# Both MLPs of a two-block model as one level of Strassen's scheme

## What is computed

```python
# first block
m = rmsnorm(h, norm_mlp[i])
h = h + jnp.square(jax.nn.relu(m @ w_up[i])) @ w_down[i]          # 1024 x 4096, 4096 x 1024
gate = jax.nn.sigmoid(rmsnorm(h, norm_ple[i]) @ w_ple_gate[i])
h = h + gate * (p[i] @ w_ple_proj[i])
# second block
h2 = rms_norm(x, norm_mlp_g[l])
x = x + jnp.square(jax.nn.relu(h2 @ w_up[l])) @ w_down[l]
```

## Time and profile before

| what | value |
|---|---|
| median of 3 runs | 2806.08 us (2803.96 to 2809.75) |
| profiled execution, its own time | 2805.16 us |
| its span | 2803.4 us |
| mean granted TensorE clock | 0.988 |
| TensorE busy | 2681.8 us, 96% |
| DVE, ACT, POOL busy | 1376.1, 601.4, 1122.2 us |
| HBM read, written | 123.36, 8.39 MB |

### The profile page before, as it was taken

How to read it: one execution, slowest core, us unless ns; L and a number is a source line. 1 busy time by engine, 2 the same in 40 slices (tenths; PEclk the granted TensorE clock), 3 DMA queues, 4 the chain that set the end, 5 groups by cost and what they waited for, 6 DMA issues and landing times.

```text
span 2803.4 us, 32575 instructions
## 1 busy us (share of the span) xinstructions
PE 2681.8 (96%) x13042; PEld 2207.0 (79%) x13042; DVE 1376.1 (49%) x1457; ACT 601.4 (21%) x713; POOL 1122.2 (40%) x617
## 2 busy tenths in 40 slices
PE   7889999899999999999998999999999999999997
PEld 6657787787788888888876788887778888888885
DVE  5677456554533322333457576667664323333234
ACT  3253313322201100011213233333232001110001
POOL 4312212223554545444444433333444545454442
PEclk9999999999999999999999999999999999999998
DMA  4200000211111111111211210001201111111111
GB/s 157 62 16 23 23 15 22 68 31 38 45 45 53 45 52 45 52 45 48 66 45 38 101 36 30 30 30 50 78 31 53 45 53 45 52 45 52 45 49 72
DMA packets 37322, 135.46 MB, mean 48 GB/s; under 512 B 4352, under 2 KB 4608, under 8 KB 37120
## 3 DMA queue, kind: packets, MB, share of 16 engines
q1 hardware_dynamic: 32112, 116.69, 13.1%
q10 hardware_dynamic: 5136, 17.70, 1.9%
HBM read 123.36 MB, written 8.39 MB: 47 GB/s over the span
## 4 chain that ended last, share of the span: by engine, by line
PE 84%; DVE 10%; ACT 3%; issue 2%; DMA 1%; SPq 0%; DVEq 0%; ACTq 0%
PE pairs L365 71%; PE mid L365 12%; DVE work L1127 3%; DVE res L1127 2%; ACT res L808 1%; DVE x_lo L1127 1%; ACT tmp L808 1%; ACT work L808 1%; DVE x_lo L1146 1%; DVE res L1636 1%; DVE tmp L1127 1%; DMA res<-x_t 0%; DVE stat L1229 0%; DVE res L1224 0%; DVE res L1552 0%
## 5 line engine op out<-in xcount | busy, mean ns | idle before, releaser
L365 PE MATMUL pairs<-x_hi,w_hi 128*128 128x512 f32 x2192 | 707.1, 404 | 55.4 <-DVE x_lo L1146 20.1
L344 POOL TENSOR_TENSOR idle<-idle 128x1 f32<-128x1 f32 x204 | 59.8, 293 | 1624.1 <-PE pairs L365 1610.2
L365 PE MATMUL pairs<-x_lo,w_hi 128*128 128x512 f32 x2192 | 684.3, 394 | 0.0
L365 PE MATMUL pairs<-x_hi,w_lo 128*128 128x512 f32 x2192 | 681.6, 393 | 0.0
L345 POOL TENSOR_SCALAR w_hi<-w_raw 128x1024 fp32r<-128x1024 f32 x204 | 571.8, 2803 | 0.0
L365 PE MATMUL pairs<-hid,w_hi 128*128 128x512 f32 x2112 | 565.5, 390 | 4.1 <-DVE work L1500 4.1
L365 PEld LDWEIGHTS pairs<-x_hi,w_hi 128*128 128x128 f32 x2192 | 402.0, 190 | 155.7 <-issue 59.4
L347 POOL TENSOR_TENSOR w_lo<-w_raw,w_hi 128x1024 fp32r<-128x1024 f32 x204 | 498.2, 2442 | 17.0
L365 PEld LDWEIGHTS pairs<-x_lo,w_hi 128*128 128x128 f32 x2192 | 412.9, 189 | 86.5
L365 PEld LDWEIGHTS pairs<-x_hi,w_lo 128*128 128x128 f32 x2192 | 412.4, 189 | 86.9
L365 PEld LDWEIGHTS pairs<-hid,w_hi 128*128 128x128 f32 x2112 | 397.2, 188 | 87.1 <-DVE work L1500 4.5
(11 more groups left out here) (157 smaller groups left out, 1798.4 us busy)
## 6 DMA issues: line engine op xcount, KB each, us to landing
w_raw<-w_stream SPq DMA_DIRECT2D x205, 512.0 KB, 3.5
res<-x_t SPq DMA_DIRECT2D x8, 512.0 KB, 10.2
work<-x_t ACTq DMA_DIRECT2D x8, 512.0 KB, 4.7
h_spill<-res ACTq DMA_DIRECT2D x8, 512.0 KB, 3.8
work<-h_spill ACTq DMA_DIRECT2D x8, 512.0 KB, 4.8
out_t<-res SPq DMA_DIRECT2D x8, 512.0 KB, 3.0
work<-res ACTq DMA_DIRECT2D x20, 128.0 KB, 2.4
work<-p_t ACTq DMA_DIRECT2D x1, 1024.0 KB, 4.8
```

Of the source, the lines that this page charges most:

```text
L344: nc.gpsimd.tensor_tensor(idle[:, 0:1], idle[:, 1:2], idle[:, 1:2], ALU.add)
L365: return nc.tensor.matmul(out, w, x, start=start, stop=stop)
```

## The change

Up and down are each treated as a product of 2x2 quadrants: the weights in four quadrants (input halves by output halves), the activations in four (channel halves by token halves). Instead of 8 products of quadrants there are 7, of sums and differences. `U_ORDER` and `D_ORDER` give their order.

- **Start.** The first 2 up units stay as they are (a pair of hidden tiles, "pair 0"). While TensorE does them, ACT and DVE make from `res` the activation operands T1 to T4 (4 tiles of 128x512 each, hi and lo): 8 scalings (`t_base`), 16 differences, 16 hi, 16 lo.
- **Up**, 15 pairs of hidden tiles, 7 steps each. A step is 12 matmuls of 128x512 into one bank; the banks go round in eight (`bank`). Its weight operand is a 128x512 piece, loaded or summed by DVE (`up_sum`, 4 a pair); ACT writes its hi, POOL its lo, in four half slots. The prefetch is four steps ahead. DVE adds the products to four accumulators (`quad`, in `tmp`), does relu times r_tok, ACT squares; DVE forms 4 sums of the 4 hidden tiles, and SP stores the 7 operands in `h_ops` in DRAM.
- **Down**, 4 chunks of 28 steps (7 products by 4 output tiles). SP loads an operand (1 MB) from h_ops and four quadrants of weights (1 MB each) a chunk; ACT and DVE split each operand in hi and lo piece by piece (`down_pieces`), DVE makes 16 sums of weights, and adds each step's bank once or twice into res and quad.
- The loops of the MLPs are written out. In POOL's split of the MLPs there is no TENSOR_SCALAR any more: the hi is ACT's. The lo of p is now POOL's. Elsewhere some semaphores are merged, with the same waits.

The added lines of its core (the functions removed stand above in whole):

```diff
+NPAIR = FF // (2 * P)
+DCH = 4
+U_ORDER, D_ORDER = (1, 7, 5, 6, 2, 3, 4), (1, 2, 6, 5, 3, 7, 4)
+U_STEPS, D_STEPS = 7 * (NPAIR - 1), 28 * DCH
+STEPS = U_STEPS + D_STEPS
+A11, A12, A21, A22 = range(4)
...
+        T1_HI, T1_LO = fours(work_r, 4), fours(work_r, 6)
+        T2_HI, T2_LO = fours(work_r, 8), fours(work_r, 10)
+        T3_HI, T3_LO = fours(work_r, 0), fours(work_r, 2)
+        T4_HI, T4_LO = x_hi[:, 0:4, RIGHT], x_lo[:, 0:4, RIGHT]
+        UP_X = {1: (x_hi[:, 0:4, LEFT], x_lo[:, 0:4, LEFT]), 2: (x_hi[:, 4:8, LEFT], x_lo[:, 4:8, LEFT]),
+                3: (x_hi[:, 4:8, RIGHT], x_lo[:, 4:8, RIGHT]), 4: (T4_HI, T4_LO), 5: (T1_HI, T1_LO),
+                6: (T2_HI, T2_LO), 7: (T3_HI, T3_LO)}
+        OP_A, OP_B, OP_C = (T3_HI, T3_LO), UP_X[2], (T2_HI, T2_LO)
+        DOWN_X = (OP_A, OP_B, OP_C, OP_A, OP_B, OP_A, OP_C)
+        H_RAW = (out_sq[:, 0:4, LEFT], x_lo_raw[:, 0:4, LEFT])
+        W_RAW = (fours(work, 4), fours(work, 6), out_sq[:, 4:8, RIGHT], x_lo_raw[:, 4:8, RIGHT])
+        S1_DOWN = x_lo_raw[:, 0:4, RIGHT]
...
+        def bank(g):
+            return mid[:, g % 8, :] if g % 8 < 4 else pairs[:, g % 8 // 2 - 2, (g % 2) * HALF:(g % 2 + 1) * HALF]
...
+        def weight_source(u0, g):
+            if g < U_STEPS:
+                return (up_raw(u0, A11), w_sum[:, :], up_raw(u0, A21), up_raw(u0, A11), up_raw(u0, A12), w_sum[:, :],
+                        up_raw(u0, A22))[g % 7]
+            q, m = divmod((g - U_STEPS) % 28, 4)
+            return (W_RAW[A11], W_RAW[A12], W_RAW[A11], S1_DOWN, W_RAW[A12], W_RAW[A21], W_RAW[A22])[q][:, m, :]
...
+        def down_pieces(n):
+            c, q, m = n // 28, n % 28 // 4, n % 4
+            o = 7 * c + q + 1
+            if q == 4:
+                return [(o + m // 2, 2 * (m % 2)), (o + m // 2, 2 * (m % 2) + 1)]
+            if q == 5 or m >= 2 or o == 7 * DCH:
+                return []
+            return [(o, 2 * m), (o, 2 * m + 1)]
...
+                def load_h(o):
+                    c, q = divmod(o, 7)
+                    p = D_ORDER[q]
+                    sp.wait_ge(h_stored[p], 16 * (b * NPAIR + 4 * c + 4))
+                    if o < 2:
+                        sp.wait_ge(s["step_done"], b * STEPS + LAST_PAIR + 1)
+                    else:
+                        sp.wait_ge(s["h_lo"], (b * 7 * DCH + o - 1) * 4)
+                    sp.dma_start(H_RAW[o % 2], h_ops[p - 1, :, 4 * c:4 * c + 4, :]).then_inc(h_raw_in[o % 2], 16)
...
+                for i in range(1, NPAIR):
+                    g = b * STEPS + 7 * (i - 1)
+                    if i < NPAIR - 1:
+                        sp.wait_ge(s["part_lo"], g + 4)
+                        sp.wait_ge(s["up_sum"], (b * (NPAIR - 1) + i) * 4)
+                        load_up(i + 1, A21)
+                        load_up(i + 1, A11)
+                        sp.wait_ge(s["part_lo"], g + 5)
+                        load_up(i + 1, A12)
+                        store_rest(i - 1)
...
+            def mlp(b, u0):
+                for g in range(STEPS):
+                    pool.wait_ge(s["part_hi"], b * STEPS + g + 1)
+                    nc.gpsimd.tensor_tensor(half_slot(w_lo, u0, g), weight_source(u0, g), half_slot(w_hi, u0, g),
+                                            ALU.subtract).then_inc(s["part_lo"], 1)
+            units(2, U_PROJ)
+            mlp(0, U_MLP1)
+            pool.wait_ge(s["ple_hi"], 1)
+            nc.gpsimd.tensor_tensor(work_r[:, 6:8, :], work[:, 14:16, :], work_r[:, 4:6, :],
+                                    ALU.subtract).then_inc(s["ple_split"], 1)
+            pool.wait_ge(s["step_done"], STEPS - 2)
+            split(0, (U_PROJ // 2 + 1) * 16, U_PROJ, U_PROJ)
+            split(1, (U_PROJ // 2 + 1) * 16, U_PROJ + 1, U_PROJ + 1)
+            units(U_PROJ + 2, UNITS - 1)
...
+                def step(g, x, ready):
+                    pe.wait_ge(s["part_lo"], b * STEPS + g + 1)
+                    whi, wlo = half_slot(w_hi, u0, g), half_slot(w_lo, u0, g)
+                    hi, lo = x
+                    out = bank(g)
                     for j in range(4):
+                        if ready is not None:
+                            pe.wait_ge(*ready(j))
+                        cols = slice(j * P, (j + 1) * P)
+                        mm(out, whi[:, cols], hi[:, j, :], j == 0, False)
+                        mm(out, whi[:, cols], lo[:, j, :], False, False)
+                        ins = mm(out, wlo[:, cols], hi[:, j, :], False, j == 3)
+                    ins.then_inc(s["step_done"], 1)
...
+                for i in range(1, NPAIR):
+                    for k, p in enumerate(U_ORDER):
...
+                        bank_read(7 * (i - 1) + k)
+                        step(7 * (i - 1) + k, UP_X[p], ready)
+                for c in range(DCH):
+                    for q in range(7):
+                        o = 7 * c + q
+                        for m in range(4):
+                            ready = (lambda j: (s["h_lo"], (b * 7 * DCH + o) * 4 + j + 1)) if m == 0 else None
+                            bank_read(step_index(c, q, m))
+                            step(step_index(c, q, m), DOWN_X[q], ready)
...
+                    if g == 0:
+                        act.wait_ge(unit_started, u0 + 2)
+                    elif g < 4:
+                        act.wait_ge(s["up_full"], 2 * (b + 1))
+                    elif U_STEPS <= g < U_STEPS + 4:
+                        act.wait_ge(s["step_done"], g0 + U_STEPS - (1, 0, 3, 2)[g - U_STEPS])
+                    else:
+                        act.wait_ge(s["step_done"], g0 + g - 3)
+                    a(half_slot(w_hi, u0, g), weight_source(u0, g), ACT.Copy, s["part_hi"])
...
+                act.wait_ge(acc_done, (n + 1) * KT)
+                t_base(0)
+                t_base(1)
+                t_hi(0)
+                t_base(2)
+                t_hi(1)
+                t_base(3)
                 norm_factor(n, e)
+                t_hi(2)
+                part_hi(0)
+                t_hi(3)
+                part_hi(1)
+                part_hi(2)
+                part_hi(3)
...
+                for g in range(STEPS):
+                    i, k = 1 + g // 7, g % 7
+                    if g < U_STEPS and k == 0:
+                        act.wait_ge(s["step_done"], g0 + g + 1)
+                        if i > 1:
+                            act.wait_ge(s["up_h"], (b * NPAIR + i) * 4 - 2)
+                        a(quad[0], bank(g), ACT.Copy, s["snap"])
+                    for ahead in {U_STEPS - 4: (), U_STEPS - 3: (), U_STEPS - 2: (2,), U_STEPS - 1: (2, 3),
+                                  U_STEPS: (3, 4)}.get(g, (4,)):
+                        if g + ahead < STEPS:
+                            part_hi(g + ahead)
...
+                def relu_r(i, k, src, dst):
+                    nc.vector.scalar_tensor_tensor(dst, src, 0.0, r_tok[:, RIGHT if k in (0, 2) else LEFT],
+                                                   ALU.max, ALU.mult).then_inc(s["up_y"], 1)
...
+                        dve.wait_ge(s["snap"], quads + i)
+                        dve.wait_ge(s["up_h"], (b * NPAIR + i) * 4)
+                        tt(quad[1], quad[0], bank(g + 3), ALU.add, s["up_step"])
+                        dve.wait_ge(s["up_step"], n + 1)
+                        tt(quad[2], quad[1], bank(g + 2), ALU.add, s["up_step"])
+                        dve.wait_ge(s["up_step"], n + 2)
+                        tt(quad[3], quad[2], bank(g + 1), ALU.add, s["up_step"])
...
+                    elif k == 4:
+                        tt(quad[0], quad[0], bank(g + 4), ALU.add, s["up_step"])
+                        dve.wait_ge(s["up_step"], n + 5)
+                        relu_r(i, 1, quad[0], quad[0])
+                        if i < NPAIR - 1:
...
+                    tt(s1, w21, w22, ALU.add, s["down_sum"])
+                    tt(w21, w11, w21, ALU.subtract, s["down_sum"])
+                    dve.wait_ge(s["part_lo"], g0 + step_index(c, 0, m) + 1)
+                    dve.wait_ge(s["down_sum"], n + 1)
+                    tt(w11, s1, w11, ALU.subtract, s["down_sum"])
...
+                    if q == 0 and c == 0:
+                        dve.wait_ge(s["up_h"], (b + 1) * NPAIR * 4 - (2, 0, 1, 3)[m])
+                        nc.vector.tensor_copy(quad[m], bank(g)).then_inc(s["down_add"], 1)
+                    elif q in (0, 2):
+                        add(quad[m], s["down_add"])
+                    if q in (0, 1):
+                        add(c11, s["down_add"])
+                    elif q in (3, 4):
+                        add(c12, s["down_add"])
+                    elif q in (5, 6):
+                        add(c21, s["down_add"])
+                    if q in (3, 5):
+                        add(c22, s["down_add"])
...
+                for d in range(D_STEPS):
+                    c, q, m = d // 28, d % 28 // 4, d % 4
+                    down_step(c, q, m)
+                    if d == 0:
+                        h_sums(NPAIR - 1)
```

(12 more changed lines are left out.)

715 lines of the change are left out of this document (495 added, 220 removed).

## The result

The changed kernel takes **2743.71 us** (median of 4 runs, 2742.22 to 2746.4) against 2806.63 for the kernel before (2803.96 to 2809.75): a ratio of 0.9779, 95% interval 0.9767 to 0.979. It is faster by 62.9 us, where 125 were forecast. The profiled execution took 2746.4 us, its span is 2744.6. One of the four executions of e9_queues_lock, further down, ran at a granted clock of 0.376 and took 6743.59 us, and it is left out of that kernel's median.

The account below looks back on a forecast made before the run. TensorE, busy 96% of the span, was taken to bound the kernel. Profiled 2805.2 - 168.7 (matmuls) + 31 (starts) + 3 (changes to down) + 8 (down) + 2 (end of MLP 1) = 2680.5; median 0.9 above: 2681 us, range 2655 to 2745.

Parts of the forecast that it names:

- The gain term: Both MLPs: 744 matmuls fewer at 0.2267 us each, -168.7 us if TensorE keeps its pace.
- Rival E: Every step: semaphore waits and 12 products into one bank lose 0.1 us at each of 434 steps, 2724 us; chance 0.05.
- The start of an MLP: Each MLP's start: TensorE stands 14 us for the first weight parts, plus 1.5 of slow clock; +31 us for two.
- Up, "Cost: 0": Pairs of up: DVE, POOL and ACT work fits beside TensorE's 19.0 us a pair, so no added time.
- six us of lateness are free: Up: prefetch four steps ahead lets ACT, POOL or DVE be some 6 us late without cost.
- The change to down: From up to down: some 3 MB must land in 10 us, about 1.5 us late, +3 us for two.
- Down, "8 us": Chunks of down: the lock between DVE and POOL makes a wait of about 1 us in each of 8, +8 us.
- Rival B: Down: DVE's queue falls behind, 5 us in each of 8 chunks, and starts of 20 us: 2722, or 2762; chance 0.20.
- C: Down from its first chunk: DVE and POOL work in series, 94.1 us a chunk: 2816, with up 2909; chance 0.07.
- The end of MLP 1: Behind MLP 1: POOL's split of p and next unit make a pause of 6 us for 4, +2 us (0 to 8).
- A POOL TENSOR_SCALAR does not lock either: POOL and DVE: this form doesn't exclude DVE's two-tile operations, by a DVE addition of 1.47 us inside one of 2.77.
- Rival D: Better: turns at the starts overlap (13 us), no chunk waits (8), changes to down cost nothing (5): 2655; chance 0.10.

Follow-up runs that it names:

- e9_queues_lock: Edits of e1_loads, e2_change and e6_base together on the changed kernel, plus e4_no_lock's copy (output not the reference's): 2673.3 us.
- e4_no_lock: Changed kernel with POOL's lo part as a TENSOR_SCALAR copy of the raw piece, the hi not subtracted (output not the reference's): 2694.38 us.
- e6_base: Changed kernel with ACT making norm factor and first hi weight right behind the first operand, two scaled bases before the last square's sum: 2735.56 us.
- e1_loads: Changed kernel with SP loading pair 2's weights before pair 0's stores, and DVE summing pair 1's last weight before pair 0's relu: 2729.95 us.
- e2_change: Changed kernel with the loads of down's first operands issued ahead of the stores at the last pair of up: 2736.57 us.
- e3_end: Changed kernel with POOL splitting p after the lo of step 19 of the last chunk instead of behind the MLP: 2748.62 us.
- e10_end_pieces: Edits of e1_loads, e2_change and e6_base together, plus POOL's split of p in quarters within the last chunk's last seven steps: 2716.22 us.

## Why the prediction was half right

**The gain term was right.** 744 matmuls are gone, and a step is 2.72 us wherever it doesn't wait. Rival E (time lost to semaphores and to 12 products into one bank) is out: in e4_no_lock, TensorE is busy for 244.00 us of 244.00.

**The start of an MLP was right in size**: 13.2 and 12.9 us of pause where 14 was worked out, and 1.8 and 1.5 of clock where 1.5 was. The clock rows show the same fall to the 1.2 GHz level behind a pause as the earlier trace rows did. It stands behind the waits of 6.10 and 5.78 us as well, for which the sum had no such term, and behind the longer pause at the end of MLP 1:

```profile
1377.00:1379.00 2.00, 1.87 (x5) 1.51 (x6) 2.00 (x2) 0.95 (x1) 0.96 (x1) 0.50 0.39 86
```

The chain of waits also has the forecast order of turns: the bases of tile 2 at 726.00, of tile 3 at 731.28, then the norm, and POOL's lo at 736.86. It is one of two chains, though. e6_base took the norm and the first hi out of it, and TensorE stood for 11.3 us one step later, for the sum of weights that DVE makes behind the operands. The prediction had followed only the first.

**Up, "Cost: 0", was wrong by 30.3 us.** 24.5 of them are pairs 1 and 2. The step that failed is the sentence that six us of lateness are free. It is nearly true of a pair in the steady state and false right after the start, where nothing has been made ahead. I had worked out when pair 0's relu is ready, and had asked of it only whether its banks come free in time. I did not follow its stores in SP's queue, where the loads of pair 2 stand behind them. e1_loads gave 16.7 us of this back in these steps. The other 5.8 us are pairs 3 to 15; they vanish in e4_no_lock, so the lock makes them.

**The change to down, 1.5 us each, was 8.2 and 7.4.** The volume of 3 MB was costed and the order of issue wasn't. SP issued the first operand's load some 8 us later in its pair than it could be (e2_change), and DVE's split of it stands ahead of the additions that free banks. e2_change shows the queue's share (8.9 us less at steps 105 to 111 of both, 7.1 of the time), e4_no_lock that a DVE with a shorter lock makes up for much of it (5.5 us left of 15.6).

**Down, "8 us", was 23.9.** This was the lock (the 23.9 are gone in e4_no_lock), foreseen as a mechanism and too small by a factor of three. The estimate took the first hump of a chunk. Measured, a middle chunk costs 1.3 us at exactly that place, as forecast. The rest stands at the two ends: 1.7 and 4.3 us in the first chunk behind the change, and 7.5 and 5.2 in the last, where the code gives DVE the next stage's sums as well. I costed all chunks as the middle one. The forecast 0.8 to 1.2 us for the mean of the two-tile operations was right (0.97). Rival B was the right mechanism in the wrong place, neither 5 us a chunk nor longer starts; C is out, DVE never fell behind without end.

**The end of MLP 1, 2 us, was 12.9.** Two faults. First, was misread: the 4.11 us pause of before at 1409.71 is not the border between the MLP and the projection. It comes after the first 24 matmuls of the projection, and the border itself, at 1400.0 us and not at 1405, had no pause. So a pause of 10.26 us replaced none, and the later one is still there with 3.88. Second, what the lock would do there was put at 3 us: POOL's split of p took 5.53 us and the TENSOR_SCALAR behind it 3.81 for 2.77, while one DVE addition beside the split took 4.97. Two other orders of POOL, e3_end and e10_end_pieces, gave nothing that the times can tell. With the copy in place of the weights' subtraction a pause of 7.00 stays.

**The lock was misread for one form.** "A POOL TENSOR_SCALAR does not lock either" rests on an addition of 1.47 us at 1379.58. Alone such an addition takes 1.22, and the missing 0.25 us are the lock: it held DVE to 1379.83, 0.90 us after POOL's operation had begun. So the trace of before did not contradict the rule of the Trainium skill that the prediction set it against. For the sum this is small, but it made the copy of e4_no_lock look like a kernel without a lock, which it isn't.

Rival D had nothing for it: no term came out lower than forecast but the start, by 1.6 us in two, and the end of the program, by 2.2. The errors had one sign. Of the 62.7 us between the forecast and the time, the copy in place of the subtraction gave 49.3 back, the three changes of order 28.5, both together 70.4, with some 8 of start in it that had been forecast. e9_queues_lock, at 2673.3, lands by the forecast of 2681. That is in part luck: the forecast was made as though the queues never stood in their own way and the lock cost one us a chunk, but it also had the whole cost of the starts, of which e9 has less, and 2 us at the end of MLP 1, where e9 still has pauses of 7.09 and 3.32.

## What to carry to other kernels

When a change makes room on the busiest engine by giving work to the others, the steady state may well fit, and did here. The cost collects at the transitions: the first pairs, the change of phase, the last chunk, the next stage. Cost those one at a time, and for each write down every in-order queue with what stands in front of what; a store that waits for a late tile holds the loads behind it as surely as a wait does.

Where two engines exclude each other, ask of a proposed order not only whether it takes work from the critical engine, but which operations of the other it will now meet. And check of a pause which instruction is on both sides of it before taking it as the border of a stage.
